# Two attention blocks in fp32 on one core: a loop written out, weight tiles in halves, later statistics, earlier bank returns

## The reference

```python
def first_block(x, ...):                       # DEPTH = 1, only the sliding window mixer is used
    x = x + swa_sink_mixer(rms_norm(x, swa_norm[0]), swa_w_in[0], ...)
# swa_sink_mixer: q, k, v, gate = split(h @ w_in)      32 query heads, 4 key/value heads of 64
#   q, k rms-normed per head; window of 128 tokens; T5 bias by distance; one sink per head
#   out = softmax(q k^T * scale + bias, sink) v, times sigmoid-gated gate, then @ w_out
def second_block(x, meta, ...):                # 16 meta tokens are put in front
    u = rms_norm_2(h, norm_w)
    sb_q, sb_k, sb_v, sb_g, df_q, df_k, df_v, df_g = split(u @ w_in)     # 8 heads of 128 each
    # df: q and k as two halves of 64, rms-normed, partial rope on 16 of 64 dims,
    #     softmax(half 0) - lam * softmax(half 1), causal, times v, then a norm per head
    # sb: stick breaking attention: exp(log_sigmoid(z) + suffix sum of log_sigmoid(-z)), times v
    # both times silu(gate), then @ w_out, added to x
```

## Time and profile before

| | |
|---|---|
| median of 3 runs | 2011.69 us (2009.98 to 2012.39) |
| time of the profiled execution | 2015.65 us |
| its span | 2014.0 us |
| mean granted TensorE clock | 0.986 |
| first block's units | about 114 to 627 us |
| first output projection | about 630 to 816 us |
| second block's heads | about 818 to 1820 us |
| second output projection | about 1823 to 2012 us |

### The profile page before, as it was taken

The page is one execution under the profiler, slowest core; times in us unless marked ns, Lnnn a source line. Parts: engine busy times, 40 slices in busy tenths (PEclk is TensorE's granted clock), DMA queues, the critical chain, the costliest instruction groups (busy, mean ns, idle before and its releaser), DMA issues.

```text
span 2014.0 us, 28665 instructions
## 1 busy us (share of the span) xinstructions
PE 1928.9 (96%) x9868; PEld 1547.7 (77%) x9868; DVE 921.3 (46%) x2325; ACT 828.4 (41%) x1831; POOL 36.2 (2%) x65
## 2 busy tenths in 40 slices
PE   4999999898998999999999999999999999988999
PEld 3777777676776888878788887888878888766887
DVE  4355555555556333544445444454444445444222
ACT  5355455454555332534335343343433435244221
POOL 1000000000000000000000000000000000000000
PEclk9999999999998999999999999999999999989999
DMA  6932223122224445322222222222222322204553
GB/s 149 203 89 70 72 74 87 55 82 60 81 55 115 126 140 148 86 66 83 65 68 80 64 64 66 81 67 77 65 66 65 83 62 64 64 21 121 132 144 83
DMA packets 298414, 173.34 MB, mean 86 GB/s; under 512 B 23040, under 2 KB 289824, under 8 KB 297824
## 3 DMA queue, kind: packets, MB, share of 16 engines
q1 hardware_dynamic: 292976, 157.55, 29.1%
q0 software_dynamic: 4352, 13.98, 2.6%
q10 hardware_dynamic: 1024, 1.07, 0.3%
HBM read 156.86 MB, written 14.66 MB: 85 GB/s over the span
## 4 chain that ended last, share of the span: by engine, by line
PE 73%; ACT 9%; DVE 7%; issue 7%; DMA 3%; ACTq 1%; DVEq 0%; SPq 0%
PE G L448 58%; PE S L710 2%; ACT wh L853 2%; ACT p L940 2%; PE G L547 2%; DMA raw<-in_swa_w_in 1%; PE O L727 1%; PE S L755 1%; PE O L783 1%; ACTq L1113 1%; ACT pT L949 1%; ACT st L942 1%; PE T L701 1%; PE G L672 1%; DVE st L1352 1%
## 5 line engine op out<-in xcount | busy, mean ns | idle before, releaser
L448 PE MATMUL G<-xh,wh 128*128 128x512 f32 (+1 forms) x2624 | 898.0, 374 | 7.8 <-DVE xl L1424 4.8
L448 PE MATMUL G<-xl,wh 128*128 128x512 f32 (+1 forms) x2624 | 845.8, 354 | 0.0
L448 PE MATMUL G<-xh,wl 128*128 128x512 f32 (+1 forms) x2624 | 842.7, 353 | 0.0
L1270 DVE TENSOR_TENSOR wl<-raw,wh 128x512 fp32r<-128x512 f32 x528 | 353.8, 688 | 550.8 <-ACT wh L853 539.1
L448 PEld LDWEIGHTS G<-xh,wh 128*128 128x128 f32 x2624 | 465.8, 190 | 107.8 <-issue 36.0
L448 PEld LDWEIGHTS G<-xh,wl 128*128 128x128 f32 x2624 | 462.9, 189 | 70.1
L448 PEld LDWEIGHTS G<-xl,wh 128*128 128x128 f32 x2624 | 463.1, 189 | 66.0 <-issue 6.9
L853 ACT ACTIVATE wh<-raw 128x512 fp32r<-128x512 f32 x528 | 313.0, 619 | 190.8 <-DMA raw<-in_w_out 97.4
L1147 ACT ACTIVATE att<-att,st 128x144 f32<-128x144 f32 (+3 forms) x64 | 36.9, 576 | 187.9 <-DVE wmeta L1609 103.3
L940 ACT ACTIVATE p<-p,st 128x256 f32<-128x256 f32 (+1 forms) x128 | 60.8, 475 | 124.6 <-DVE st L1339 124.6
L1339 DVE CUSTOM_DVE_ANT_0 p<-S,bias,sink_u 128x256 f32<-128x256 f32 (+1 forms) x128 | 56.1, 442 | 0.0
(11 more groups left out here) (216 smaller groups left out, 1699.2 us busy)
## 6 DMA issues: line engine op xcount, KB each, us to landing
raw<-in_w_in SPq DMA_DIRECT2D x56, 1024.0 KB, 6.0
raw<-in_swa_w_in SPq DMA_DIRECT2D x32, 1024.0 KB, 5.5
raw<-in_swa_w_out SPq DMA_DIRECT2D x16, 1024.0 KB, 6.2
raw<-in_w_out SPq DMA_DIRECT2D x16, 1024.0 KB, 6.4
raw<-in_w_in POOLq DMA_DIRECT2D x8, 1024.0 KB, 7.4
rel_rows<-relb SPq DMA_DIRECT2D x1, 6128.0 KB, 36.7
mixed<-in_x SPq DMA_DIRECT2D x4, 1024.0 KB, 10.0
raw<-in_swa_w_in SPq DMA_DIRECT2D x8, 512.0 KB, 7.2
```

The lines of the kernel that those rows point to most:

```text
L448: mm = pe.matmul(d, w[:, slot, k, :], v[:, k, a:b], start=(k == 0 and n == 0), stop=(k == KC - 1 and n == 2))
L1270: V.tensor_tensor(wl[:, slot, q, :], raw[:, slot, q, :], wh[:, slot, q, :].bitcast(F32), ALU.subtract).then_inc(w_lo, 1)
```

## The change

Four edits. (1) The loop over i = 1 to 3 of the first block is a Python loop on all five queues, so its twelve units are written out like the first four. (2) `weights` loads a tile as two DMAs of 8 chunks each, the first when two quarters of the tile two before have been split, the second when all four have. The first half counts on `raw_in[slot]`, the second on a new `raw_late[slot]`, for which ACT waits before the third quarter. The gate tiles use `weights` too; key/value tiles and `SBQ` stay whole. (3) In the second block the chain of dfq and dfk runs one point later from PE's statistics on: PE 1 to 2, ACT 2 to 3 and 4 to 5, DVE 3 to 4 and 6 to 7. (4) PE takes the banks of dfq and dfk again when ACT's Ln has read them (`n_ln`), and those of dfg and sbg when DVE has taken the product out (`e_raw`), instead of waiting for `used`.

```diff
@@ sync
             def weights(tile, slot, w_v, col):
-                after(sp, w_lo, 4 * (tile - 2) + 4)
-                sp.dma_start(raw[:, slot, :, :], w_v[:, :, ds(col, P)]).then_inc(raw_in[slot], 16)
+                for part, s in enumerate((raw_in[slot], raw_late[slot])):
+                    c = slice(part * KC // 2, part * KC // 2 + KC // 2)
+                    after(sp, w_lo, 4 * (tile - 2) + 2 * part + 2)
+                    sp.dma_start(raw[:, slot, c, :], w_v[:, c, ds(col, P)]).then_inc(s, 16)
...
                 weights(T_UNIT + 2 * u, 0, w1_v, P * (4 * g + i))
-                after(sp, w_lo, 4 * (T_UNIT + 2 * u - 1) + 4)
-                sp.dma_start(raw[:, 1, :, :], w1_v[:, :, ds(SWA_GATE + P * (4 * g + i), P)]).then_inc(gate_in, 16)
+                weights(T_UNIT + 2 * u + 1, 1, w1_v, SWA_GATE + P * (4 * g + i))
...
-            with sp.Fori(1, UNITS) as i:
+            for i in range(1, UNITS):
...
@@ gpsimd, tensor, scalar, vector: the same line of the loop
-            with pe.Fori(1, UNITS) as i:
+            for i in range(1, UNITS):
...
@@ tensor, finish
-                    if p == 1:
+                    if p == 2:
                         norm_stat(two, 2 * h + ti + 1)
@@ tensor, head
                     for owner, back in OWNERS2[name]:
-                        after(pe, used[owner], h + 1 - back)
+                        if owner in ("dfq", "dfk"):
+                            after(pe, n_ln, 2 * (h - back) + (1 if owner == "dfq" else 2))
+                        elif owner in ("dfg", "sbg"):
+                            after(pe, e_raw, 2 * (h - back) + (1 if owner == "dfg" else 2))
+                        else:
+                            after(pe, used[owner], h + 1 - back)
@@ scalar, split
+                if quarter == 2 and loaded[0] is raw_in[slot] and len(loaded) == 2:
+                    act.wait_ge(raw_late[slot], loaded[1] - KV_LOADS)
                 if quarter == 0:
-                    act.wait_ge(*loaded)
+                    act.wait_ge(*loaded[0:2])
@@ scalar, finish
-                    if p == 2:
+                    if p == 3:
                         after(act, n_stat, count)
...
-                    if p == 4:
+                    if p == 5:
                         buf, width = (dfk, ALL) if ti else (dfq, TOK)
@@ vector, finish
-                    if p == 3:
+                    if p == 4:
                         after(dve, n_rs, count)
...
-                    if p == 6:
+                    if p == 7:
                         after(dve, n_rot, 64 * count)
```

More of the change, by code:

```diff
@@ L193, in build @@
         raw_in = [sem(f"raw_in{i}") for i in range(2)]
-        gate_in, sbq_in = sem("gate_in"), sem("sbq_in")
+        raw_late = [sem(f"raw_late{i}") for i in range(2)]
+        sbq_in = sem("sbq_in")
         mats_in, c_in, c2_in, m_in, x_in = sem("mats_in"), sem("c_in"), sem("c2_in"), sem("m_in"), [sem(f"x_in{t}") for t in range(NB)]
@@ L418, in _ @@
                 sinks_of(0, g)
-            with pool.Fori(1, UNITS) as i:
+            for i in range(1, UNITS):
                 for g in range(KV):
@@ L825, in _ @@
             KV_LOADS = 2 * 16 * (KV // 2)
-            OUT1_LOADS = (KV_LOADS + 16 * 4 * UNITS, KV_LOADS)
+            OUT1_LOADS = (KV_LOADS + 16 * 4 * UNITS, KV_LOADS + 16 * 4 * UNITS)
             HEAD_LOADS = tuple(n + 16 * (KC // 2) for n in OUT1_LOADS)
@@ L830, in kv_loaded @@
             def kv_loaded(g):
-                return (raw_in[g % 2], 32 * (g // 2 + 1)) if g < KV else unit_loaded(0, 0)
+                return (raw_in[g % 2], 32 * (g // 2 + 1), "whole") if g < KV else unit_loaded(0, 0)
             def unit_loaded(u, half):
-                return (gate_in, 16 * (u + 1)) if half else (raw_in[0], KV_LOADS + 16 * (u + 1))
+                return raw_in[half], KV_LOADS + 16 * (u + 1)
             def out_loaded(loads, i, slot):
@@ L998, in _ @@
                 swa_window(0, g, attend=g > 0)
-            with act.Fori(1, UNITS) as i:
+            for i in range(1, UNITS):
                 for g in range(KV):
@@ L1414, in _ @@
                 swa_window(0, g, attend=g > 0)
-            with dve.Fori(1, UNITS) as i:
+            for i in range(1, UNITS):
                 for g in range(KV):
```

## The result

The changed kernel takes **1985.37 us** (median of 4 runs, 1983.83 to 1988.27) against 2012.01 us (median of 4, 2009.98 to 2012.39): a ratio of 0.9871 with a 95% interval of 0.9855 to 0.9887, 26.6 us faster. The forecast was 1987.7 us, range 1979 to 1998: off by 2.3 us. The profiled execution took 1983.83 us (span 1982.1).

What follows compares the result with a forecast made beforehand. TensorE, busy 96% of the span, was taken as the bound, so edits win only where it idles. Terms 11.7 + 1.5 + 6.9 + 2.4 + 1.5 = 24.0 us, off the median 2011.69, gave 1987.7 us, range 1979 to 1998.

Steps and rivals of the forecast that it cites:

- Part 1: First block: writing out the loop removes jumps and register arithmetic on all five queues, gaining 11.7 us over eleven units.
- the signs named: First block: eleven units at 32.0 us, no DVE "issue" pause over 1 us, no clock fall before 590 us, among others.
- the rival: First block: the loop's gain is not had, as with fetch pauses in long code; 1993.6 or 1999.4 us, chance 0.10.
- Part 2: First unit's first tile: half transfers land the first 512 KB sooner, gaining 1.5 us (bounds 0 to 2.8); nothing in steady state.
- Part 3: Looped heads 1 to 7: statistics one point later remove PE's 0.83 us wait, gaining seven times 0.99, 6.9 us.
- part 4: Second block: banks given back at the last read remove two waits in head 0, 2.4 us; worth nothing in looped heads.
- The clock term: Second block's heads: a clock fall after the tiny meta-score matmuls costs 1.5 us; one fall fewer than six, 1.5 us.
- The rivals: Later chain stalls PE elsewhere 0.14, loop's gain not had 0.10, clock falls vanish 0.10, halves make transfers the bound 0.04.
- one rival: Second block's heads: the clock falls vanish, up to 7.5 us more than counted, 1980 us; chance 0.10.
- the bound: Output projections: halves needing over 5.8 us each make transfers the limit; at 6.4 us each, 2024 us; chance 0.04.

Runs made afterwards that it cites:

- part 4 alone: Only the banks of the second block given back at their last read, against the kernel before: 2016.89 us, ratio 1.0.
- part 3 alone: Only the chain of dfq and dfk moved one point later, banks still given back at the rotation's end, against the kernel before: 2043.75 us, ratio 1.0142.

## Why the prediction was right, and where it was not

- **Part 1 was right in place and nearly in size.** Forecast 11.7 us, measured 11.1 from unit to unit between the two profiles, and 10.4 for the whole kernel by itself. The pause of 5.07 us on DVE was rightly read as the loop's jump: putting DVE's loop alone back brings a pause back (3.1 to 3.2 us, beside the lighter traffic), and the four other loops together add 2.0 us. No DVE pause on "issue" over 1 us and no clock fall is left from the start of the units to 590 us, which were two of the signs named; before, the clock also fell to half behind both jumps (0.51 over 358.2 to 361.2, 0.50 over 491.7 to 494.7). Written-out code brought no pause, as the rival would have had it. Single units of 32.2 to 32.3 us remain at the same places in every kernel with the written-out loop; their cause is open.
- **Part 2's place was right, its price too low.** "With halves the first 512 KB should land half of the remaining 2.9 us sooner: 1.5 us gained": it landed 2.1 us sooner by ACT's first split, and PE's wait fell by 2.0. What the step lacked is a clock fall behind the long wait, in the five other profiles with whole transfers, which makes the part worth some 3 to 6 us (114.2 to 114.45 us to the first unit's statistics in three of them and 116.6 in two, with halves 110.5 to 111.4). Why the execution in hand had no fall is open. Neither did it foresee that the early half shortens DVE's pause by 1.9 us, since less weight traffic is under way at the jump. That effect is void once the loop is written out, which is why the parts don't add: 0.58% for the loop, 0.32% for the halves and 0.68% for the heads make 1.58%, where the full change gives 1.29%. Counted twice in that sum are the jump units' 3.5 us (0.17%); the rest of the gap is inside the intervals.
- **Part 3 was right in mechanism, under-sized.** Nothing took the stall's place, with the margin at `later_l` that was worked out (0.93 and 0.95 us to the row before it). The term was 0.99 us a head, measured 1.39. The distance between the statistics of dfq and of dfk shrank from 17.60 to 17.47 us, and that from there to the next head's from 104.12 to 102.84 (without a fall): more than the stall of 0.83 and the 0.16 for what overlaps. The other 0.4 us lie around the statistics' new places: from start to start, the six statistics matmuls of a head take 1.16 us instead of 1.94, and the projections' matmuls together 0.4 more. Why they run faster there wasn't tested.
- **"In the looped heads PE never waits for a bank, so it is worth nothing there" failed.** It holds for part 4 alone, with the statistics where they stood before, and the runs show it there (ratio 1.0). But part 3 moves the rotation to point 7, and the old release of the bank hangs on the rotation. Had the parts been costed in pairs, the step would have been: without part 4, part 3 costs 28 us (waits of 31.1 us at the banks, and clock falls behind six of them), so part 4 is worth some 40 us beside it. The forecast for the sum came out right because both were in it.
- **The clock term had the right price and a poor count.** A fall costs 1.50 us as worked out (121.81 less 120.31), but three went, not one. The fewer falls go with the changed heads: all six profiles that have both parts 3 and 4 and the tiny matmuls in one run have three falls in the seven looped heads, while five of those without both parts have four to seven (six before, five with the loop alone and with both halves late, four with the halves alone, seven with the banks alone). The sixth, part 3 alone, has three at this place and six more behind the bank waits. Which heads have a fall is not explained here; that the tiny meta-score matmuls bring it about is, by their split.
- **The sum, and where it was luck.** By its steps the forecast gave 24.0 us; between the two profiled executions 31.8 us were gained, 7.8 more. The medians are only 26.6 us apart, since the profiled execution of before lay 3.6 us above its median and that of after 1.5 us below. So the miss of 2.3 us is smaller than the errors of the terms. All but one lay on the same side (start 0.8, head 0 0.3, heads 2.8, clock 3.0, ends 1.5, against the loop's 0.6), and where the two profiled executions lay against their medians took most of them back. With part 3 alone rightly sized, the forecast would have been 1984.9.
- **The rivals.** None came whole; of the falls that one rival let vanish, half went. Halves land in 3.6 to 5.1 us by the medians of their groups (4.7 in the last projection), under the 5.8 at which they would have become the bound, and PE's projection tiles are unchanged at 11.57 us.

## What to carry to other kernels

When several edits touch one chain, cost each of them with and without the others: a resource given back earlier can be worth nothing by itself and still be what another edit stands on. Before a hardware loop is kept around long bodies, look for pauses with the releaser "issue" on each engine at the jump; here one queue of five carried 5.6 us of the loop's cost and the other four together 2.0, and the pause grew with the DMA traffic beside it. A run of tiny matmuls counts as busy and still precedes a fall of the clock; in these heads it helped to put full ones in its middle.

## What the runs showed of the hardware that was not expected

- The pause of DVE at a loop's jump depended on the DMA traffic at that moment: 5.04 and 5.07 us with 305 and 301 GB/s in its first three microseconds, 3.1 to 3.2 us with 105 to 124 GB/s. The packet that fetches instructions started 2.8 us into the long pauses and 1.0 to 1.1 us into the short ones, as the weights ran out. A second pause of 1.4 to 1.6 us follows.
- 16 matmuls of 16 columns in 2.18 us, on an engine that counts as busy all the time, were followed by half the clock in three of seven heads of the full change and in six of seven before; with six full matmuls in their middle, in none of seven, in two kernels.
- PE's idle stretch of 2.2 to 2.8 us at the start of the first block was followed by half the clock in five of the six profiles that have it, and PE's wait of 2.6 us for a bank in six of seven looped heads with the later statistics alone.
- A DMA that writes rows from 16 partitions ran at 102 GB/s where one from 32 partitions ran at 205 GB/s, so that half the data took 34.2 and 43.1 us against 36.7; that the number of partitions is the reason was not tested by itself.
